# Compression of keys and values cut in three, with quarters of a weight group between the parts, and the log gates set behind the third quarter

## What is computed

```python
proj = h @ w_in[l]                       # 512 x 1024 by 1024 x IN_WIDTH, split into 15 pieces
log_a = jax.nn.log_sigmoid(a_lr @ w_alpha2 + b_alpha) / GLA_TAU      # rank 16 to 512: the log gates
b = jnp.cumsum(heads(log_a, GLA_DK), axis=3)                         # running sums in chunks of 64
...
def compress(t, pe, w1, w2):             # for n_kc and n_vc, 31 blocks of 32 tokens, stride 16
    blocks = t[:, :, idx_c] + pe
    flat = blocks.reshape(B, G, n_cmp, L * DH)
    return jax.nn.silu(flat @ w1) @ w2   # w1: 32*64 x 64, w2: 64 x 64, for 2 groups
```

## Time and profile before

| | us |
|---|---|
| median of 3 runs | 1486.6 (1486.48 to 1488.46) |
| the profiled execution, its time | 1488.3 |
| the profiled execution, its span | 1486.5 |
| TensorE busy | 1474.9 |
| VectorE busy | 661.8 |
| ScalarE busy | 584.8 |
| GpSimd busy | 653.1 |
| mean granted clock of TensorE | 0.995 |

### The profile page before, as it was taken

The page is one execution under the profiler, slowest core; times in us unless marked ns, Lnnn a source line. Parts: engine busy times, 40 slices in busy tenths (PEclk is TensorE's granted clock), DMA queues, the critical chain, the costliest instruction groups (busy, mean ns, idle before and its releaser), DMA issues.

```text
span 1486.5 us, 20009 instructions
## 1 busy us (share of the span) xinstructions
PE 1474.9 (99%) x7268; PEld 1187.7 (80%) x7268; DVE 661.8 (45%) x1077; ACT 584.8 (39%) x919; POOL 653.1 (44%) x304
## 2 busy tenths in 40 slices
PE   9999999999999999999999999999999999999999
PEld 7888788878878877888888886777768888888887
DVE  5313545676543376333331107988755343332000
ACT  5233332765562344322332225665654233332211
POOL 4433311663244434444444442666234444444543
PEclk9999999999999999999999999999999999999999
DMA  5522211111123322222233333321122323332333
GB/s 198 169 72 79 83 51 42 55 46 58 58 71 100 99 76 95 99 97 89 96 99 103 110 101 114 125 72 58 43 72 86 102 95 99 99 99 96 103 103 124
DMA packets 38494, 135.05 MB, mean 91 GB/s; under 512 B 4496, under 2 KB 4752, under 8 KB 38176
## 3 DMA queue, kind: packets, MB, share of 16 engines
q1 hardware_dynamic: 37248, 130.70, 26.7%
q10 hardware_dynamic: 1184, 3.51, 0.7%
HBM read 132.09 MB, written 2.10 MB: 90 GB/s over the span
## 4 chain that ended last, share of the span: by engine, by line
PE 77%; issue 14%; DVE 5%; POOL 4%; ACT 0%; DMA 0%; POOLq 0%; SPq 0%; DVEq 0%; ACTq 0%
PE bank L1136 17%; PE bank L1137 17%; PE bank L1138 17%; POOL wL L477 3%; PE bank L1490 3%; PE bank L1491 2%; PE bank L1492 2%; PE bank L1165 2%; PE bank L1167 2%; PE bank L1166 2%; PE bank L1266 1%; DVE bank L2192 1%; PE bank L1267 1%; PE bank L1268 1%; PE bank L1545 1%
## 5 line engine op out<-in xcount | busy, mean ns | idle before, releaser
L477 POOL TENSOR_TENSOR wL<-raw,wH 128x1024 fp32r<-128x1024 f32 x234 | 573.4, 2450 | 779.7 <-ACT wH L573 634.6
L573 ACT ACTIVATE wH<-raw 128x1024 fp32r<-128x1024 f32 x209 | 221.3, 1059 | 601.2 <-PE bank L1138 528.3
L1136 PE MATMUL bank<-aH,wH 128*128 128x512 f32 x920 | 359.8, 391 | 1.1 <-POOL wL L477 1.1
L1137 PE MATMUL bank<-aL,wH 128*128 128x512 f32 x920 | 358.0, 389 | 0.0
L1138 PE MATMUL bank<-aH,wL 128*128 128x512 f32 x920 | 358.0, 389 | 0.0
L1136 PEld LDWEIGHTS bank<-aH,wH 128*128 128x128 f32 x920 | 172.7, 188 | 40.6 <-POOL wL L477 1.9
L1138 PEld LDWEIGHTS bank<-aH,wL 128*128 128x128 f32 x920 | 172.7, 188 | 36.1
L1137 PEld LDWEIGHTS bank<-aL,wH 128*128 128x128 f32 x920 | 172.7, 188 | 35.7 <-issue 0.5
L1137 PE MATMUL bank<-fL,wH 128*128 128x512 f32 x352 | 137.0, 389 | 0.0
L1136 PE MATMUL bank<-fH,wH 128*128 128x512 f32 x352 | 137.0, 389 | 0.0
L1138 PE MATMUL bank<-fH,wL 128*128 128x512 f32 x352 | 136.9, 389 | 0.0
(11 more groups left out here) (333 smaller groups left out, 2022.0 us busy)
## 6 DMA issues: line engine op xcount, KB each, us to landing
raw<-in_w SPq DMA_DIRECT2D x234, 512.0 KB, 3.3
bmk<-in_bias SPq DMA_DIRECT2D x6, 512.0 KB, 4.5
out_x<-xT SPq DMA_DIRECT2D x8, 256.0 KB, 4.3
xT<-in_x SPq DMA_DIRECT2D x3, 512.0 KB, 6.8
ct<-in_ct ACTq DMA_DIRECT2D x3, 384.0 KB, 3.9
w1k<-in_w1k ACTq DMA_DIRECT2D x1, 1024.0 KB, 6.3
w1v<-in_w1v ACTq DMA_DIRECT2D x1, 1024.0 KB, 4.8
xT<-in_x SPq DMA_DIRECT2D x2, 256.0 KB, 3.5
```

What stands on the lines that cost most here:

```text
L477: pool.tensor_tensor(wL[:, c_slot, :], raw[:, c_slot, :], wH[:, c_slot, :].bitcast(F32), ALU.subtract).then_inc(sem("w_lo"), 1)
L573: act.activation(wH[:, s, :], raw[:, s, :], ACT.Copy).then_inc(sem("w_hi"), 1)
L1136: pe.matmul(bank[:], hi, H[:, ka, :], start=(k == 0), stop=False)
L1137: pe.matmul(bank[:], hi, L[:, ka, :], start=False, stop=False)
```

## The change

The first layer of the compression becomes a function over a running number from 0 to 63 (input, then position; two products for each), called for 0 to 21, 22 to 42 and 43 to 63. Behind each part stands a quarter of group 4. The two log gates come behind the third quarter, and the fourth quarter behind them. ScalarE prepares chunks 18 and 19 ahead of the silu, chunk 20 ahead of the log gates' activations, and chunk 21 between the two sets of keys. VectorE's memset of `attnT` goes behind the taking out of group 4. No operation is added or taken away, and no wait; their places change.

```diff
@@ scalar
             group(p, 12)
+            group(p, 16, 2)
             act.wait_ge(sem("cmp_hid"), 1)
             for i in range(2):
                 act.activation(hid[:, i, :], B[7][:, i * 64:i * 64 + NCMP], ACT.Silu).then_inc(sem("hid_ready"), 1)
             act.preload_act_table_set("natural_log_exp_and_others")
...
+            group(p, 18, 1)
             log_gate(0)
             log_gate(1)
-            group(p, 16, 2)
             act.wait_ge(sem("kin_ready"), 4)
             act.wait_ge(sem("v_S"), 2)
             high_of_keys(0)
+            group(p, 19, 1)
             high_of_keys(1)
-            group(p, 18, 2)
             group(p, 20)
@@ tensor
-            def values_by_token(g):
+            def values_by_token(g, ks=range(KD)):
-                for k in range(KD):
+                for k in ks:
...
-            for i, w1 in enumerate((w1k, w1v)):
-                for l in range(CL):
+
+            def hidden_of_blocks(a, b):
+                for n in range(a, b):
+                    i, l = n // CL, n % CL
                     for g in range(NG):
                         r = slice(g * DH, (g + 1) * DH)
-                        mm = pe.matmul(B[7][r, i * 64:i * 64 + NCMP], w1[r, l, :], kin[i][r, l, :],
+                        mm = pe.matmul(B[7][r, i * 64:i * 64 + NCMP], (w1k, w1v)[i][r, l, :], kin[i][r, l, :],
                                        start=(l == 0), stop=(l == CL - 1))
-            mm.then_inc(sem("cmp_hid"), 1)
+                return mm
+            hidden_of_blocks(0, 22)
+            values_by_token(4, range(0, 2))
+            hidden_of_blocks(22, 43)
+            values_by_token(4, range(2, 4))
+            hidden_of_blocks(43, 2 * CL).then_inc(sem("cmp_hid"), 1)
+            values_by_token(4, range(4, 6))
...
             log_gate(0)
             log_gate(1)
-            values_by_token(4)
+            values_by_token(4, range(6, KD))
@@ vector
             log_gate(0)
             log_gate(1)
+            values_by_token(4)
             dve.memset(attnT[:], 0.0).then_inc(sem("attn_zero"), 1)
-            values_by_token(4)
```

## The result

The changed kernel took 1490.48 us (median of 17 runs, 1489.06 to 1491.74), the kernel before 1486.91 us (median of 17, 1485.32 to 1490.65). The ratio is 1.0018, with a 95% interval of 1.0011 to 1.0024: 1.6 to 3.6 us slower. The forecast of 1485.0 had the sign wrong, and the median lies above the range's end of 1488.4.

A forecast was written before the change was run, and what follows sets the result against it. Bound by TensorE's speed, not waits: 7.58 + 16.32 + 0.60 + 1.91 + 5.68 + 1.05 + 0.91 = 34.05 us against 35.61, 1.56 less, taken off the 1486.6 median: 1485.0 us, range 1482.8 to 1488.4.

The forecast's parts named there:

- the base of the sum: First compression product to first product of group 5: 35.61 us before, from one profile, set against 34.05 after.
- the full clock behind the stall: TensorE keeps 2.4 GHz through the interleaving and a second-layer stall of 0 to 2 us; chance 0.45.
- the low clock of before: Half clock in the log gates and group 4 behind the compression costs 3.2 us, which the change wins back.
- switches: TensorE changing between small products, dense products and log gates in the interleaved stretch: 0.60 us in all.
- the wait: Second layer on TensorE stalls for VectorE's scans of both gates: about 1.05 us, bounds 0 to 2.0.
- The second rival: Clock falls anyway, at the log gates or the stall with four small products behind it: 1486.6 or 1487.2 us; chance 0.22.
- The third rival: Clock falls after each of three compression parts, 1.6 us per fall: 1489.8 us, slower by 0.2%; chance 0.08.
- The fourth rival: Work after the change starts 1.6 us earlier, so one later fall, as at 1026.0, is gone: 1483.4 us; chance 0.13.
- the weights: Group 4's weight chunks, prepared earlier on ScalarE, are ready before TensorE wants them: no wait.
- second wait: VectorE's taking out of group 4, needed by group 5, has one tile ready after 0.7 us: no further TensorE wait.
- the silu and tables: The silu and its two table loads lie under the third quarter of group 4: cost nothing.
- the gates: The pair of log gates on TensorE, behind the third quarter, takes 1.91 us at full clock.

The follow-up runs named there:

- uncut_gates_after_q1: Kernel before, compression still in one piece, but one quarter of group 4 put between it and the log gates; 1487.32 us, ratio 0.9994.
- the two cut versions: Changed kernel with the log gates right behind the last compression part: three parts 1488.6 us (1.0004 to before), five parts 1489.35 us (1.0013).

## Why the prediction was wrong

**Two steps failed: the base of the sum, and the full clock behind the stall.** In its own terms the prediction had -3.2 for the low clock of before, +0.60 for switches and +1.05 for the wait, and nothing for a new fall: -1.55 us. The runs give -2.0, +0.94, +1.64 and +1.6: +2.2 us. Of the 3.7 us between the two, 1.6 are the new fall, 1.2 the base, 0.6 the wait and 0.3 the switches. With the base alone put right the sum would still have been slightly negative.

**The base.** "That low stretch is all that the change can win back here", and "Together 3.2 us": the prediction took the low clock of one profiled execution for a property of the kernel. Four profiles put its cost at 0 to 3.2 us, 2.0 in the mean. The gain to be had was 2 us, and in some executions nothing. The comparison of the timed runs (two near 1486.5, one 1.9 above) was at hand. The prediction called the 1.9 us about the cost of one fall, and yet took its whole gain, worked out from an execution of 1488.3 us with a long fall, off the median of 1486.6.

**The sum at full clock** has no gain in it, only costs, and they add up from profiles of other kernels: base 32.41, gates apart 0.21 (uncut_gates_after_q1), two more pairs of switches 0.7 to 0.77 (the two cut versions), wait 1.6, together 34.9 to 35.0 against 34.99 and 35.05 measured. That is 2.6 us more than before at full clock.

**Switches**, 0.60 predicted, about 0.94 measured (34.99 - 32.41 - 1.64; the 1.64 are the 1.96 us from the last product of the fourth quarter to the second layer, less the 0.32 of before). Most of the missing third is at the change from compression to dense: the first part took 2.68 us to the next dense start where 44 products at 59 ns give 2.60, and three such changes make about 0.25 us. I had taken the row of the second layer for it, inside bounds of 0 to 0.3.

**The wait**, 1.05 predicted, 1.57 measured, inside its bounds of 0 to 2.0. Its place, cause and order were right. The model was the third gate, whose instruction has one wait; the first gate's has two, and that costs the 0.5 us. The trace of before showed it, in the gap from 107.26 to 107.80 that I did not read.

**The clock behind the wait.** The second rival named the place ("the stall with the four small products of the second layer behind it, 2 us together") and the price of 1.6 us; it had 0.22. The sum itself had it at nothing. In six profiles of kernels with the wait the fall came five times, and it cost 1.6 us (1354.42 against 1352.79 of the rest). It takes back most of the 2.0 us that are saved in the mean where before has its low clock: 2.6 + 1.6 - 2.0 = 2.2 us, which is inside the measured 1.6 to 3.6. This sum rests on four profiles of before and two of the changed kernel, so its clock terms are rough; the 2.6 are not.

**The third rival**, a fall behind each part, did not occur: no profile of the changed kernel had the clock below 1.00 in its parts or in the first three quarters. The Trainium skill's second failure mode ("TensorE: Matmul & The Clock Gate") is about short pauses of TensorE between groups of products; applied to the cuts, as the prediction did, it would have had the clock swing with each. It did not with five parts. The new fall came behind an idle time of TensorE of 1.1 to 2.9 us and the four small products, which is nearer to what the same page says under "Why this matters for your kernels", where it ties falls to idle gaps. The falls of before do not agree with that: they came behind 7.6 us of uninterrupted small products and log gates.

**The fourth rival**, shifted later falls, plays a part in single executions. The fall near 1025 us was there in eleven of fourteen profiles, among them both of the changed kernel, and missing once in before; it gives no direction. The one near 900 us was in three of four profiles of before and in neither of the changed kernel, worth about 0.4 us.

**What held:** the weights were always in time, the taking out of group 4 caused no second wait, the silu and tables were hidden, and the gates took 1.91 us.

## What to carry to other kernels

One profile shows one execution. Before a low-clock stretch is booked as a gain to be had, look at it in a second and third execution, and make the sum at full clock apart: if it has only costs, the change lives on chance. Small work taken apart costs a fixed price per switch, here 0.35 to 0.38 us a pair. Dense work between two small stages did better here than dense work inside one (32.62 us for the stretch, no fall in two profiles). When a producer is moved later, follow its whole chain over the other engines to the consumer, and read the gaps of that very chain in the old trace, not those of its twin.

## What the runs showed of the hardware

- An instruction of VectorE with two waits, one long met, started 0.54 us after the event that it waited for; with one wait, 0.03 us after.
- A subtraction of VectorE on 128x512 took 2.04 us beside a subtraction of GpSimd on 128x1024 that had started 1.0 us before it, and 0.69 us alone.
- The same program, in four profiled executions, had no low clock, 3.4 us of it, or 6.8 us of it twice, behind the same 7.6 us of small products and with the two log gates next to them.
- A fall of 3.4 us in dense products cost 1.6 us of time (1354.42 against 1352.79 us for the rest of the span).
- The time up to the first compression product varied by 2.6 us over fourteen profiled executions, and by 2.25 us (95.96 to 98.21) over four of the same program.
